# First stage of a two-layer block in eight chunks of 256 + 256 columns, with the column sums taken from held weights

## The reference, cut to what matters

```python
c_act = jax.nn.silu(c)
mod = c_act @ w_ada + b_ada                       # (2048) @ (2048, 12288)
sh_a, sc_a, gt_a, sh_f, sc_f, gt_f = split(mod, 6)
h = _rmsnorm(x, norm_mix) * (1.0 + sc_a) + sh_a   # x: (256, 2048)
p = h @ w_in                                      # (2048, 9296): c_q 512, c_kv 512, k_pe 64, q, k, v, ...
```

## Time and profile before

| | |
|---|---|
| median of 3 runs | 2284.07 us |
| profiled execution | 2282.7 us |
| its span | 2281.4 us |
| TensorE busy | 2227.9 us (98%) |
| DVE busy | 1518.0 us (67%) |
| ACT busy | 1020.2 us (45%) |
| moved by DMA | 506.75 MB, mean 222 GB/s |
| mean granted TensorE clock | 0.996 |

### The profile page before, as it was taken

One profiled execution on the slowest core, in us unless ns is written; L12 is line 12 of the kernel. 1 busy time (PEld: TensorE's weight loads), 2 busy tenths in 40 slices (PEclk: granted clock), 3 DMA queues, 4 the chain that ended last, 5 costly groups with the idle time before them and its releaser, 6 DMA issues.

```text
span 2281.4 us, 27025 instructions
## 1 busy us (share of the span) xinstructions
PE 2227.9 (98%) x10783; PEld 1855.8 (81%) x10783; DVE 1518.0 (67%) x1947; ACT 1020.2 (45%) x1286; POOL 24.5 (1%) x28
## 2 busy tenths in 40 slices
PE   5999999999999999999999999999999999999998
PEld 3678998888887888888888888887888888888886
DVE  5888998887759767765544555466556565655556
ACT  4345454333444464443344434456444444434444
POOL 0000000000000000000000000000000000000000
PEclk9999999999999999999999999999999999999999
DMA  9966867585778868865555565555565555555553
GB/s 363 381 241 207 275 218 260 189 285 185 240 278 296 286 237 281 275 236 195 193 194 184 185 203 185 192 194 194 188 200 189 189 189 189 189 186 195 198 190 131
DMA packets 276445, 506.75 MB, mean 222 GB/s; under 512 B 24032, under 2 KB 38112, under 8 KB 275296
## 3 DMA queue, kind: packets, MB, share of 16 engines
q1 hardware_dynamic: 276320, 505.03, 65.3%
HBM read 502.51 MB, written 2.49 MB: 221 GB/s over the span
## 4 chain that ended last, share of the span: by engine, by line
PE 82%; DVE 8%; DMA 4%; ACT 2%; issue 2%; SPq 1%; POOL 0%; DVEq 0%; ACTq 0%
PE bank L1204 25%; PE bank L1206 25%; PE bank L1205 25%; DVE WL L1941 3%; PE bank L1397 2%; DMA RAW<-in_w_o_dram 2%; DVE GA L1922 1%; ACT WH L1486 1%; PE bank L1125 1%; DMA A<-in_w_ada_dram 1%; PE bank L1216 1%; PE bank L1217 1%; PE bank L1218 1%; DVE A L2168 1%; DMA A<-in_w_in_dram 1%
## 5 line engine op out<-in xcount | busy, mean ns | idle before, releaser
L1941 DVE TENSOR_TENSOR WL<-RAW,WH 128x1024 fp32r<-128x1024 f32 (+1 forms) x714 | 865.0, 1219 | 592.4 <-ACT WH L1486 588.5
L1486 ACT CAST WH<-RAW 128x1024 fp32r<-128x1024 f32 (+1 forms) x714 | 745.3, 1050 | 889.4 <-PE bank L1206 718.3
L1204 PE MATMUL bank<-WH,HTh 128*128 128x512 f32 x1936 | 764.6, 395 | 7.5 <-DVE WL L1941 6.9
L1206 PE MATMUL bank<-WH,HTl 128*128 128x512 f32 x1936 | 754.3, 390 | 0.0
L1205 PE MATMUL bank<-WL,HTh 128*128 128x512 f32 x1936 | 753.8, 389 | 0.0
L1204 PEld LDWEIGHTS bank<-WH,HTh 128*128 128x128 f32 x1936 | 363.6, 188 | 86.8 <-DVE WL L1941 11.1
L1206 PEld LDWEIGHTS bank<-WH,HTl 128*128 128x128 f32 x1936 | 363.4, 188 | 76.6
L1205 PEld LDWEIGHTS bank<-WL,HTh 128*128 128x128 f32 x1936 | 363.7, 188 | 74.7 <-issue 1.9
L1922 DVE SCALAR_TENSOR_TENSOR GA<-RAW,ST,GA 128x512 f32<-128x512 f32 x264 | 181.2, 748 | 13.5 <-DMA RAW<-in_w_ada_dram 7.8
L1204 PE MATMUL bank<-WH,R2h 128*128 128x512 f32 x408 | 161.4, 396 | 2.8 <-DVE WL L1941 2.8
L1206 PE MATMUL bank<-WH,R2l 128*128 128x512 f32 x408 | 159.6, 391 | 0.0
(11 more groups left out here) (280 smaller groups left out, 1784.0 us busy)
## 6 DMA issues: line engine op xcount, KB each, us to landing
RAW<-in_a_w_in_dram SPq DMA_DIRECT2D x96, 1024.0 KB, 5.1
RAW<-in_w_gate_up_dram SPq DMA_DIRECT2D x88, 1024.0 KB, 5.1
RAW<-in_w_ada_dram SPq DMA_DIRECT2D x80, 1024.0 KB, 5.3
RAW<-in_w_in_dram SPq DMA_DIRECT2D x63, 1024.0 KB, 5.0
RAW<-in_w_down_dram SPq DMA_DIRECT2D x44, 1024.0 KB, 5.0
RAW<-in_a_w_out_dram SPq DMA_DIRECT2D x32, 1024.0 KB, 5.0
A<-in_w_ada_dram SPq DMA_DIRECT2D x16, 1024.0 KB, 11.7
RAW<-in_w_o_dram SPq DMA_DIRECT2D x16, 1024.0 KB, 5.2
```

What stands on the lines that cost most here:

```text
L1204: e.matmul(o, ah[:, s], hi[:, k, :], start=first, stop=False)
L1206: i = e.matmul(o, al[:, s], hi[:, k, :], start=False, stop=last)
L1486: e.copy(hi, rv).then_inc(S["hi"], 1)
L1941: e.tensor_tensor(lo, rv, hi.bitcast(F32), ALU.subtract).then_inc(S["lo"], 1)
```

## The change

- `CHUNKS` has eight chunks of 256 shift and 256 scale columns. One chunk gives two tiles of `h`. A "g" unit is two DMAs with runs of 1 KB. A w_in load of this stage is 2 tiles, 0.5 MB, and one half. In the list, the four jobs follow each chunk with an eighth; `conv` is one further behind. The jobs of this stage may also use the two places in R2h/R2l (`EXTRA_R`).
- Step `mod`: the raw tile (2 tiles of the last quarter) or GA is the stationary operand, in blocks of 128 columns, and `cact` or a column of ones moves, one column: 16 matmuls. The sum arrives along partitions; `mod_e` is one addition. The other two tiles of the last quarter are two more L1922-type instructions on DVE.
- Step `x_rs` becomes `x_sq` (one half of x squared by ACT, the other by DVE) and `x_sc` (both scalings on DVE). In `h` the full-precision copy moves from DVE to ACT.
- `xt` stands before the first `mod`. The constants are loaded in two parts, the second at the end of the stage.

```diff
-CHUNKS = [s + 512 * c for c in range(4) for s in (2048, 0)]
+CHUNKS = [256 * c for c in range(8)]
...
-    return 10 * ci + 4 * q + 2 if ci < 8 else 80 + 14 * (ci - 8) + 4 * q + 2
+    return 12 * ci + (2, 6, 10, 12)[q] if ci < 8 else 96 + 14 * (ci - 8) + 4 * q + 2
...
+        for ci in range(8):
+            u.extend(("g", ci, q) for q in range(4))
+            u.extend(("w", j, 2 * ci, 2) for j in jobs[:4])
...
+        sm, cq, ckv, conv = jobs
+        for ci in range(8):
             for q in range(4):
...
+                self.put("ada", i, ci, q)
+                self.marks[("raw_free", self.raw_slot(i))] = ("ga_dve", ga_value(ci, q)) if q < 3 else ("mod_t", ci + 1)
...
+                if (ci, q) == (0, 0):
+                    m = self.ms()
+                    self.put("x_sq", m)
+                elif (ci, q) == (0, 1):
+                    self.put("x_sc", m)
+                elif (ci, q) == (0, 2):
                     self.put("columns")
...
                     self.put("xt")
...
+            self.put("mod", ci, None, i)
+            self.issue_loads()
+            if ci:
+                self.front_half(conv, 3)
+            self.front_split(sm)
+            self.put("mod_e", ci, None)
+            self.put("cam", ci)
+            self.front_split(cq)
+            self.put("h", ci)
+            self.front_split(ckv)
+            self.front_split(conv)
+            self.front_half(sm, 2)
+            self.front_half(cq, 0)
+            self.front_half(ckv, 1)
+        self.put("load_cst2")
+        self.put("rope_tables")
+        self.front_half(conv, 3)
...
-                    e.matmul(b, ones, L.GA[:, ci % 2, h, :], start=h == 0, stop=False)
...
-                for t in range(4):
-                    i = e.matmul(b, L.CB[:, t, :], rv[:, t, :], start=False, stop=t == 3)
+                for t in (2, 3):
+                    for m in range(4):
+                        e.matmul(b[:, m:m + 1], rv[:, t, m * P:(m + 1) * P], L.cact[:, 12 + t:13 + t],
+                                 start=t == 2 and m == 0, stop=False, skip_group_check=True)
+                W.wait_ge("ga_dve", ga_value(ci, 3))
+                W.wait_ge("cst_in", 16)
                 for h in range(2):
+                    for m in range(4):
+                        i = e.matmul(b[:, m:m + 1], L.GA[:, ci % 2, h, m * P:(m + 1) * P], ones[:, 0:1],
+                                     start=False, stop=h == 1, skip_group_check=True)
...
+            W.wait_ge("ht_lo", c - 1)
+            for kt in (2 * c, 2 * c + 1):
+                e.activation(L.tmp1[c % 2][:, kt % 2 * T:kt % 2 * T + T], L.XT0[:, kt, :], ACT.Identity,
+                             scale=L.cAm[:, kt:kt + 1], bias=L.cBm[:, kt:kt + 1]).then_inc(S["xmod"], 1)
...
+            e.tensor_tensor_reduce(out=L.XS1[:, 1, :], in0=L.X[:, 1, :], in1=L.X[:, 1, :], scale=1.0, scalar=0.0,
+                                   op0=ALU.mult, op1=ALU.add, accum_out=L.ss1[:, 1:2]).then_inc(S["xsq"], 1)
...
+                e.tensor_scalar(L.XS1[:, b, :], L.X[:, b, :], L.rs1[:, b:b + 1], None, ALU.mult).then_inc(S["xs"], 1)
...
+                src, dst = a["w_ada"].rearrange("(p t) n -> p t n", p=P)[:, 4 * q:4 * q + 4, :], L.raw(slot, 4, 512)
+                for c0, d0, n in ((0, 0, 256), (2048, 256, 256)) if ci < 8 else ((0, 0, 512),):
```

More of the change, by code:

```diff
@@ L110, in make_jobs @@
              conv(0, O_Q)]
+    for j in front:
+        j.extra = EXTRA_R
     a1 = [conv(1, O_Q + 512), conv(2, O_K)]
@@ L380, in issue_loads @@
             u, s = self.units[i], self.raw_slot(i)
-            n = 1
+            n = 2 if u[0] == "g" and u[1] < 8 else 1
             if u[0] == "w":
@@ L463, in front @@
         self.issue_loads()
-        where = {"cq": 0, "ckv": 1, "conv": 3, "sm": 2}
-        for ci in range(2):
+        sm, cq, ckv, conv = jobs
+        for ci in range(8):
             for q in range(4):
-                if ci == 0 and q == 3:
+                i = self.staged[0]
+                self.put("ada", i, ci, q)
+                self.marks[("raw_free", self.raw_slot(i))] = ("ga_dve", ga_value(ci, q)) if q < 3 else ("mod_t", ci + 1)
+                self.staged[0] += 1
+                if q < 3:
+                    self.issue_loads()
[5 more added lines that the diff above has]
+                elif (ci, q) == (0, 2):
@@ L468, in front @@
                     self.put("columns")
[L469 to L472, removed]
                     self.put("xt")
[L474 to L502, removed]
@@ L503, in front, with front_split @@
+        self.put("rope_tables")
+        self.front_half(conv, 3)
         self.have |= {("mod", ci) for ci in range(8)} | {("ht", kt) for kt in range(16)}
-    def front_unit(self):
+    def front_split(self, j):
         i = self.staged[0]
[L507 to L518, removed]
+        _, uj, t0, nkt = self.units[i]
+        assert uj is j
+        hid = len(self.halves)
+        place = self.free_place(j)
+        self.place.append(place)
+        self.after.append(self.user[place] + 1)
+        self.user[place] = hid
+        self.halves.append((j, t0, nkt, i, 0, nkt))
+        self.put("split", hid)
+        self.marks[("raw_free", self.raw_slot(i))] = ("lo", hid + 1)
@@ L519, in front_unit, with front_half @@
         self.staged[0] += 1
         self.issue_loads()
[L522 to L525, removed]
+    def front_half(self, j, where):
+        assert self.halves[self.used][0] is j
+        self.put("half", self.used, where)
+        self.used += 1
         j.end = self.used
@@ L1236, in pe_program @@
             W.wait_ge("g", 1)
+            W.wait_ge("cst_in", 32)
             take(6)
@@ L1914, in dve_program @@
             W.wait_ge("cact", 2)
-            for t in range(2 if q == 0 else 0, 4):
+            last = 1 if ci < 8 and q == 3 else 3
+            for t in range(2 if q == 0 else 0, last + 1):
                 g, col = L.GA[:, ci % 2, t % 2, :], L.cact[:, 4 * q + t:4 * q + t + 1]
-                n = ga_value(ci, q) - 3 + t
+                n = ga_value(ci, q) - last + t
                 if q == 0:
@@ L1937, in dve_program @@
             W.wait_ge("half", sch.after[hid])
-            if sch.place[hid] >= NHL:
+            if sch.place[hid] >= NHL and j.x != "ht":
                 W.wait_ge(*extra_free(sch, sch.place[hid]))
@@ L1973, in dve_program @@
         elif kind == "h":
             c, = args
-            tm = L.tmp1[c % 2]
-            W.wait_ge("cam", c + 1)
-            W.wait_ge("mod", mod_value(2 * c + 1))
-            W.wait_ge("xt_e", 2 * c + 2)
-            W.wait_ge("ht_lo", 2 * c - 2)
-            for i in range(4):
-                kt = 4 * c + i
-                e.tensor_scalar(tm[:, i * T:(i + 1) * T], L.XT0[:, kt, :], L.cAm[:, kt:kt + 1], L.cBm[:, kt:kt + 1],
-                                ALU.mult, ALU.add).then_inc(S["xmod"], 1)
@@ L1984, in dve_program @@
-            for i in range(2):
-                kt = 4 * c + 2 * i
-                W.wait_ge("ht_hi", kt + 2)
-                W.wait_ge("xmod", kt + 2)
-                e.tensor_tensor(L.HTl[:, kt:kt + 2, :], tm[:, 2 * i * T:2 * (i + 1) * T].rearrange("p (k t) -> p k t", t=T),
-                                L.HTh[:, kt:kt + 2, :].bitcast(F32), ALU.subtract).then_inc(S["ht_lo"], 1)
+            kt = 2 * c
+            W.wait_ge("ht_hi", kt + 2)
+            W.wait_ge("xmod", kt + 2)
+            e.tensor_tensor(L.HTl[:, kt:kt + 2, :], L.tmp1[c % 2].rearrange("p (k t) -> p k t", t=T),
+                            L.HTh[:, kt:kt + 2, :].bitcast(F32), ALU.subtract).then_inc(S["ht_lo"], 1)
```

101 lines of the change are left out of this document (46 added, 55 removed).

## The result

| | before | after |
|---|---|---|
| median | 2283.99 us (2283.22 to 2284.69, 4 runs) | 2294.16 us (2293.03 to 2296.81, 4 runs) |
| ratio after/before | | 1.0043, 95% interval 1.0031 to 1.0056 |
| profiled execution, its span | 2282.7, 2281.4 us | 2296.81, 2295.5 us |
| mean granted TensorE clock | 0.996 | 0.985 |
| first split of conv(1) on DVE | 154.02 | 167.63 |

The changed kernel is slower by 10 us. It is the case that the prediction called (b), not its likeliest one, which had put 2286.5.

What follows compares the result with a forecast made beforehand. DVE's in-order chain was taken as the bound: mod_e(0) 30.5, then 13.9, six loops of 16.0, 2.1, 5.9 and 8.1 give 156.5, +2.5 against 154.02, hence 2286.5 us; range 2279 to 2295.

Steps and rivals of the forecast that it cites:

- (b): Rival: TensorE's clock falls in every chunk, making the sums over GA up to 2.0 us longer; about 2293 us, chance 0.24.
- The ruler: First split of conv(1) on DVE, at 154.02 before: the program's end was taken to move by what this split moves.
- DVE's chain as the bound: First-stage loop per chunk, from DVE's last accumulate to the next chunk's: 16.0 us, of which waits are 3.2.
- B: Second half of a chunk's column sums on TensorE, against GA, behind DVE's last accumulate: 2.0 us, 2.1 with semaphores.
- the forecast's own case: First-stage loop of 15.8 to 16.3 us, end moving -1 to +6, 2283 to 2290 us; chance 0.47.
- The start: Before the first loop: x scaling ends near 19.6, transposes take 7 us, first mod_e at 30.5.
- The transfers: First-stage loads of w_ada in 1 KB runs at 368 GB/s: 15.8 us a chunk, bounds 15.2 and 16.9.
- Rival (c): First-stage loads: 1 KB runs cost as much as 512 B ones, 16.9 us a chunk; 2290 us, chance 0.08.
- The tail: After the last chunk's sums: 5.9 us to the last conv split, 8.1 for rope tables and latent norms, ending at 156.5.
- Rival (a): DVE's chain is shorter than counted and transfers alone set the pace, 15.2 to 15.4 a chunk; about 2279 us, chance 0.21.

Runs made afterwards that it cites:

- wide_sums: The changed kernel with the old column sums (wide matmuls, diagonal product and reduction on DVE) instead of the held-weight ones; 2299.84 us.
- reorder: The changed kernel with the cq split ahead of the waiting mod_e and the ckv split ahead of h's wait; 2286.39 us.
- before_rope: The kernel before, with DVE's part of the rope tables moved ahead of its wait for mod_e(1); 2283.34 us.
- warm: The changed kernel with five added 256-column matmuls into unused columns, in TensorE's gap ahead of the sums over GA; 2300.33 us.
- after_2k: The changed kernel with first-stage tiles loaded in one 2 KB run instead of two of 1 KB, computing other numbers; 2294.1 us.
- warm_2k: The kernel warm with first-stage tiles loaded in runs of 2 KB instead of 1 KB, computing other numbers; 2296.62 us.
- narrow: The changed kernel with nine added one-column matmuls in TensorE's gap ahead of the sums over GA; 2308.8 us.
- reorder_2k: The kernel reorder with first-stage tiles loaded in runs of 2 KB instead of 1 KB, computing other numbers; 2279.44 us.
- conv_between: The changed kernel with the conv half of the chunk before put between the raw-tile sums and the sums over GA; 2301.35 us.

## Why the prediction came out as it did

- **The ruler.** Right for the change: 13.6 us of split against 14.1 of span. As a rule it is weaker than stated. Between the split and the end of the span lie 2127.4 us before and 2127.9 after, but 2130.1 in `wide_sums` and 2130.7 in `reorder`, so a single trace tells the end to some 3 us only; where those come from was not followed. And it holds while DVE is late there and not TensorE, as `before_rope` shows.
- **DVE's chain as the bound, 16.0 us.** Right. The loop with B at full clock is 16.04 in the changed kernel and 15.89 in `warm`, `after_2k` and `warm_2k`. The waits are as counted: 1.80 for TensorE in that loop, and 7.5 + 1.9 us in seven loops for ACT, 1.3 each.
- **The clock, rival (b).** This is the step that failed in the forecast's own case, which counted B at 2.1 us throughout. B ran at half clock in six of seven loops, 1.5 us more in each: 7 x 17.29 is 121.0 us against 112.0 counted, so 9.0 of the excess. The rival had the place, the price (up to 2.0 a chunk) and the time (2293 for half slow, against 2294.2 measured with six of seven slow, since the measured price is below 2.0). I held against it that "shorter gaps leave the clock alone". That was wrong: the gaps were 0.70 to 1.91 us, and the clock fell. The rival's own cause was half right: it named 2.4 us of idle time with one-column matmuls around it, and `narrow` and the first B lose the clock with no idle time at all.
- **The start.** mod_e(0) at 32.72 and not 30.5, 2.2 us. B ran at half clock here as well (3.3 us instead of 2.0). The second quarter landed at 15.8 instead of 14.0, and the scaling behind it ended at 20.9 instead of 19.6; with runs of 2 KB mod_e(0) is at 30.61. The 7 us taken for the transposes were 6.8. The prediction's sentence that 3.78 us at 21.93 agree with a slow start rests on the durations alone: the trace has a granted clock of 1.00 there.
- **The transfers.** 368 GB/s for runs of 1 KB was too high. A chunk took 16.34 us at a full queue (`reorder`) and not 15.8. With w_in at 387 GB/s as forecast, 4.3 us, that leaves 12.1 us for w_ada, an estimate of 347 GB/s. It is nearer the bound of 16.9 than I chose, and 0.3 above the chain of 16.0. In the changed kernel the slow chain hid it, so it cost nothing behind the start. It is a part of what kept `warm` from its gain: with 2 KB runs its mean loop is 17.09 instead of 17.62, and the rest of the way to 15.9 is the added matmuls' (`warm_2k`). Rival (c) was thus a second limit right behind the first. By the row of the Trainium skill on line rate, 512 B and more ("DMA: Bandwidth & Descriptors", "Specifications"), 1 KB would have run as fast as 2 KB. `reorder` against `reorder_2k`, 354 against 379 GB/s from 40 to 135 us, says it does not.
- **The tail.** Right: 14.0 us counted from mod_e(7) to the split, 13.89 measured. The sum is then 2.2 + 9.0 - 0.1 = 11.1 over 156.5, the 167.6 of the trace. This is the trace of the slowest execution, 2296.81; the median is 2.65 us lower, and no trace shows where.
- **Rival (a)**, the chain shorter than counted, did not occur by itself. `reorder_2k` built it, and its 2279.44 is the 2279 that (a) gave.
- **Luck.** That the median fell into the range is owed to (b), which had a chance of 0.24, and to a range drawn to its middle; the forecast's own case, 2283 to 2290, was missed by 4 us.

One loop of seven keeps the clock, and the traces show what precedes it. In the seven chunks behind the first, B ran at full clock where TensorE's idle time ahead of it was 0.58 us, and at half where it was 0.70 to 1.91. The idle time was short because TensorE itself was late: in the chunk before, 28 records of matmuls behind B ran at half clock, up to 91 us, while in the chunks ahead of a long loop it was 11 to 16. The two short loops of `after_2k` at 15.89 have the same history, 23 and 27 such records, and idle times of 0.56 and 0.50. So a slow engine does fill its own gap, as the prediction held against (b), but only in one loop of seven. What stays open is why the half clock lasts longer in some chunks, and how few one-column matmuls are enough to lose it.

## What to carry to other kernels

In a loop where one in-order engine waits for a short job of TensorE, cost that job at half clock too, and look at what TensorE does ahead of it. Fill the waiting engine's wait with work that it has to do anyway (`reorder`, 7.8 us) before filling TensorE's gap (`warm`, `conv_between`, both slower here). When a chain is to be shortened, compute the next limit first: here the transfers stood 0.3 us behind it. A ruler taken on one engine holds only as long as that engine is the late one.

## What was not expected of the hardware

- One-column matmuls without any gap were followed by a fall of the granted clock from 1.00 to 0.50 (`narrow`, 67 to 73 us), while a gap of 2.40 us behind four records of 512 columns was not (`wide_sums`, 1.00).
- Sixteen records with a held 128x128 operand and one moving column take 1.84 to 1.95 us at full clock and up to 3.58 at half (`after`).
- A full queue with w_ada in runs of 1 KB moved 348 to 358 GB/s (`reorder`, windows of 10 us from 30 to 140), in runs of 2 KB 375 to 386 (`reorder_2k`, from 50 to 130).
